# Delta-rule heads: values from keys times state, filling work in eighths, and two reordered GpSimd steps

## The reference, cut to what matters

```python
t_inv = triangular_solve(eye + lower, eye)            # inverse of a unit triangular matrix
u = t_inv @ v_beta
w = t_inv @ (k_beta * exp(g))
def step(state, xs):
    v_new = u_c - w_c @ state
    o = q_c @ state + qk_c @ v_new
    state = state * exp(g_last) + k_c.T @ v_new
```

## Time and profile before

| What | Value |
|---|---|
| median of 3 runs | 2177.07 us |
| the profiled execution, its own time | 2178.32 us |
| its span | 2176.5 us |
| mean granted TensorE clock | 0.989 |
| PE busy over the span | 97% |
| DVE, ACT, POOL busy | 60%, 39%, 19% |
| the heads' loop and the last head | about 75 to 627 us of the span |

### The profile page before, as it was taken

One profiled execution on the slowest core, in us unless ns is written; L12 is line 12 of the kernel. 1 busy time (PEld: TensorE's weight loads), 2 busy tenths in 40 slices (PEclk: granted clock), 3 DMA queues, 4 the chain that ended last, 5 costly groups with the idle time before them and its releaser, 6 DMA issues.

```text
span 2176.5 us, 29829 instructions
## 1 busy us (share of the span) xinstructions
PE 2120.2 (97%) x10312; PEld 1735.3 (80%) x10312; DVE 1315.0 (60%) x1907; ACT 858.1 (39%) x1352; POOL 421.0 (19%) x326
## 2 busy tenths in 40 slices
PE   6999999999999999999999999999999999999998
PEld 4788888888888878888888888888777777888886
DVE  6777887777644453333557655643788867555431
ACT  3333333333332232222335454422666735545321
POOL 0456765556700300000110000011000000000021
PEclk8999999999999999999999999999999999999999
DMA  7344433344333323333332333233221122333332
GB/s 286 97 117 125 116 101 111 106 116 125 106 88 116 116 78 96 96 96 93 96 114 69 96 96 96 86 102 101 59 59 49 54 84 85 96 96 96 94 96 73
DMA packets 394815, 216.81 MB, mean 100 GB/s; under 512 B 7880, under 2 KB 391298, under 8 KB 393219
## 3 DMA queue, kind: packets, MB, share of 16 engines
q1 hardware_dynamic: 393939, 213.51, 33.3%
q0 software_dynamic: 288, 2.10, 0.3%
q10 hardware_dynamic: 528, 0.40, 0.1%
HBM read 211.79 MB, written 4.19 MB: 99 GB/s over the span
## 4 chain that ended last, share of the span: by engine, by line
PE 74%; DVE 7%; issue 7%; POOL 5%; ACT 2%; POOLq 0%; DMA 0%; ACTq 0%; DVEq 0%
PE ps L2206 23%; PE ps L2208 22%; PE ps L2207 22%; POOL ada_w L725 3%; PE ps L2382 1%; DVE small L2088 1%; DVE a_sb L2121 1%; DVE w_lo L1309 1%; POOL gd_dia L748 1%; PE ps L2233 1%; DVE a_t_lo L2097 1%; ACT at_swap L1200 1%; DVE prob L2116 1%; POOL ada_s L725 1%; ACT prob L1223 0%
## 5 line engine op out<-in xcount | busy, mean ns | idle before, releaser
L2206 PE MATMUL ps<-h_hi,w_hi 128*128 128x512 f32 x1896 | 770.4, 406 | 7.1 <-DVE h_lo L1373 5.5
L2208 PE MATMUL ps<-h_hi,w_lo 128*128 128x512 f32 x1896 | 743.6, 392 | 0.0
L2207 PE MATMUL ps<-h_lo,w_hi 128*128 128x512 f32 x1896 | 741.9, 391 | 0.0
L1309 DVE TENSOR_TENSOR w_lo<-raw,w_hi 128x1024 fp32r<-128x1024 f32 x333 | 430.0, 1292 | 355.9 <-ACT w_hi L808 355.5
L808 ACT ACTIVATE w_hi<-raw 128x1024 fp32r<-128x1024 f32 x336 | 355.6, 1059 | 636.6 <-PE ps L2208 578.3
L2206 PEld LDWEIGHTS ps<-h_hi,w_hi 128*128 128x128 f32 x1896 | 358.6, 189 | 80.2 <-issue 13.8
L2208 PEld LDWEIGHTS ps<-h_hi,w_lo 128*128 128x128 f32 x1896 | 357.5, 189 | 78.2
L2207 PEld LDWEIGHTS ps<-h_lo,w_hi 128*128 128x128 f32 x1896 | 359.0, 189 | 65.0
L2206 PE MATMUL ps<-act_hi,w_hi 128*128 128x512 f32 x528 | 206.0, 390 | 0.0
L2208 PE MATMUL ps<-act_hi,w_lo 128*128 128x512 f32 x528 | 205.5, 389 | 0.0
L2207 PE MATMUL ps<-act_lo,w_hi 128*128 128x512 f32 x528 | 205.4, 389 | 0.0
(11 more groups left out here) (383 smaller groups left out, 2599.0 us busy)
## 6 DMA issues: line engine op xcount, KB each, us to landing
raw<-ffn_w_up SPq DMA_DIRECT2D x88, 512.0 KB, 3.7
raw<-w_in SPq DMA_DIRECT2D x72, 512.0 KB, 3.7
raw<-w_ffn_in SPq DMA_DIRECT2D x44, 512.0 KB, 3.7
ada_w<-w_ada SPq DMA_DIRECT2D x32, 512.0 KB, 3.8
raw<-ffn_w_down SPq DMA_DIRECT2D x32, 512.0 KB, 3.8
raw<-diff_w_qkv SPq DMA_DIRECT2D x24, 512.0 KB, 3.7
ada<-w_ada SPq DMA_DIRECT2D x8, 1024.0 KB, 12.6
ada_w<-w_ada_f SPq DMA_DIRECT2D x16, 512.0 KB, 3.7
```

The source lines that it names most:

```text
L1309: nc.vector.tensor_tensor(w_lo[:, tile.slot], raw[:, tile.raw], w_hi[:, tile.slot].bitcast(F32), SUB)\
L2206: nc.tensor.matmul(dst, w_hi[:, tile.slot, k], hi, start=first, stop=False)
L2207: nc.tensor.matmul(dst, w_hi[:, tile.slot, k], lo, start=False, stop=False)
L2208: return nc.tensor.matmul(dst, w_lo[:, tile.slot, k], hi, start=False, stop=last)
```

## The change

- **Values.** `w`, its four matmuls, ACT's copy of it and `k_beg` go. For chunks 1 to 3, PE multiplies the keys with the state (`k_state{n}`, one f32 matmul of its own), DVE adds the result times the (negative) factor to `v_b` (`rest{n}`), and `v_new{n}` is one matmul of the inverse with that. ACT copies the keys to `k_f` after `q_squares`.
- **Filling.** It goes by eighths (3 large matmuls). The steps keep what they had, two eighths, but for `v_new0` (it had two quarters, now two eighths), `o2` and `o3` (one eighth each, had a quarter), and the new `k_state{n}` (two eighths each).
- **DVE's queue.** The short convolution's taps move to places behind the states; `ahead(4)` moves from behind the third copy to behind the fourth and `short_gate`; `ahead(5)` moves from behind the fourth copy to behind `g_col`, ahead of `ahead(6)`.
- **POOL.** The fourth mask stands ahead of the second modulation tile.
- **The start.** DVE computes `w_lo` of head 0's tile 1. POOL does `k_norm` of head 0 first, then `w_lo` of tiles 2 and 3, and DVE waits for them only ahead of `ahead(0)`. Head 0 stands outside POOL's loop.

```diff
-    DVE_STEPS += ["k_dec"] if _n == 0 else ["u_pairs3", "k_beg"] if _n == 3 else []
-PE_STEPS += [f"u{LEVELS - 1}", "w"]
-ACT_STEPS += ["w"] + [f"o_squares{_n}" for _n in range(NC)] + ["o_hi"]
+    DVE_STEPS += ["k_dec"] if _n == 0 else ["u_pairs3"] if _n == 3 else []
+PE_STEPS += [f"u{LEVELS - 1}"]
+ACT_STEPS += [f"o_squares{_n}" for _n in range(NC)] + ["o_hi"]
 for _n in range(NC):
-    PE_STEPS += [f"v_new{_n}", f"o{_n}"]
-    DVE_STEPS += [f"v_new{_n}"] + ([f"state{_n}"] if _n < NC - 1 else [])
+    PE_STEPS += ([f"k_state{_n}"] if _n else []) + [f"v_new{_n}", f"o{_n}"]
+    DVE_STEPS += ([f"rest{_n}"] if _n else []) + [f"v_new{_n}"] + ([f"state{_n}"] if _n < NC - 1 else [])
...
-HEAD_FILL = {name: 1 for name in PE_STEPS}
-HEAD_FILL.update(y0=2, v_new0=2, o_turn=3)
-LAST_FILL = dict(HEAD_FILL, y1=2, y2=2, y3=2, y4=2, y5=2, v_new0=2, v_new1=2, v_new2=2, ada_turns=2)
+HEAD_FILL = {name: 2 for name in PE_STEPS}
+HEAD_FILL.update(y0=4, o2=1, o3=1, o_turn=6)
+LAST_FILL = dict(HEAD_FILL, y1=4, y2=4, y3=4, y4=4, y5=4, v_new0=4, v_new1=4, v_new2=4, ada_turns=4, o_turn=4, tail=16)
...
-            for tile in [QKVZ.tile(t, 0).ahead() for t in range(1, 4)]:
+            def first_splits():
+
+                for t in (2, 3):
...
                 nc.gpsimd.tensor_tensor(col4(S_KN), col4(S_KSS), minus_half, ALU.pow).then_inc(g_pool, 1)
+                if splits is not None:
+                    splits()
...
-                    if n in (1, 2):
-                        modulation(n - 1)
+                    if n in (1, 3):
+                        modulation(n // 2)
...
+                nc.scalar.activation(gd["k_f"][:], gd["k_s"][:], ACT.Copy).then_inc(g_act, 1)
...
-                after_pe("w")
-                nc.scalar.activation(gd["x_t"][:], bank(7), ACT.Copy).then_inc(g_act, 1)
...
+            split(QKVZ.tile(1, 0).ahead())
             z_silu(QKVZ, 3, 0, 0)
-            dve.wait_ge(lo_ready, QKVZ.tile(3, 0).ahead().before + 1)
...
                 for n in range(NC):
+                    if n:
+                        after_pe(f"k_state{n}")
+                        own("v_beta")
+                        nc.vector.scalar_tensor_tensor(part(gd["v_b"], n), part(bank(7), n), small[:, S_KBEG + n:S_KBEG + n + 1],
+                                                       part(gd["v_b"], n), MULT, ADD).then_inc(g_dve, 1)
                     after_pe(f"v_new{n}")
                     nc.vector.tensor_copy(part(gd["y_t"], n), part(bank(2), n)).then_inc(g_dve, 1)
                     if more and n == 0:
                         short_in()
-                        short_tap(0)
-                    if more and n == 1:
-                        short_tap(2)
-                    if more and n == 2:
-                        ahead(4)
-                    if more and n == 3:
-                        ahead(5)
...
-                    if more and n == 0:
-                        short_tap(1)
-                    if more and n == 1:
+                    if more and n < 3:
+                        short_tap(n)
+                    if more and n == 3:
                         short_gate()
+                        ahead(4)
...
                 if more:
+                    ahead(5)
                     ahead(6)
...
-                fill("w")
-                after_act(f"u{LEVELS - 1}")
...
-                by_chunk(7, gd["k_beg"], u_t).then_inc(g_pe, 1)
-
                 for n in range(NC):
+                    if n:
+                        fill(f"k_state{n}")
+                        after_dve(f"state{n - 1}")
...
+                        nc.tensor.matmul(part(bank(7), n), part(gd["k_f"], n), state[:], start=True, stop=True).then_inc(g_pe, 1)
                     fill(f"v_new{n}")
-                    v_new = nc.tensor.matmul(part(bank(2), n), part(u_t, n), part(gd["v_b"], n), start=True, stop=n == 0)
                     if n:
-                        after_act("w")
-                        after_dve(f"state{n - 1}")
-                        v_new = nc.tensor.matmul(part(bank(2), n), part(x_t, n), state[:], start=False, stop=True)
+                        after_dve(f"rest{n}")
+                    else:
+                        after_act(f"u{LEVELS - 1}")
+                    v_new = nc.tensor.matmul(part(bank(2), n), part(u_t, n), part(gd["v_b"], n), start=True, stop=True)
```

More of the change, by code:

```diff
@@ L172 @@
              "u_diag", "x_pairs", "qk"]
-ACT_STEPS = ["k_squares", "exp_decay", "exp_g", "exp_g_rows", "exp_last", "exp_left", "q_squares"]
+ACT_STEPS = ["k_squares", "exp_decay", "exp_g", "exp_g_rows", "exp_last", "exp_left", "q_squares", "k_copy"]
 POOL_STEPS = ["k_norm"] + [f"mask{_n}" for _n in range(WHOLE_LEVELS)] + ["low_pairs", "ada", "o_norm"]
@@ L348, in block_kernel @@
         names = ["q_s", "k_s", "v_s", "z_g", "th", "cc", "dec", "low_d", "low", "q_g", "u_t", "x_t",
-                 "y_t", "k_beg", "k_dec", "v_b", "dia"]
+                 "y_t", "k_f", "k_dec", "v_b", "dia"]
         gd = {n: sb("gd_" + n, [P, T], at=work + 2048 * j) for j, n in enumerate(names)}
@@ L711, in _, with head @@
             factor(N_MIX)
-            pool.wait_ge(g_dve, 1)
-            for tile in [QKVZ.tile(t, 0).ahead() for t in range(1, 4)]:
[L715 to L720, removed]
+            def first_splits():
+                for t in (2, 3):
+                    tile = QKVZ.tile(t, 0).ahead()
+                    pool.wait_ge(hi_ready, tile.before + 1)
+                    pool.wait_ge(lo_ready, tile.before)
+                    nc.gpsimd.tensor_tensor(w_lo[:, tile.slot], raw[:, tile.raw], w_hi[:, tile.slot].bitcast(F32), SUB)\
+                      .then_inc(lo_ready, 1)
+            def head(h, splits=None):
                 own = [24 * h + 1]
@@ L767, in _ @@
             pool.sem_inc(ada_own, 1)
-            with pool.Fori(0, H) as h:
+            head(0, first_splits)
+            with pool.Fori(1, H) as h:
                 head(h)
@@ L1060, in head @@
                                          accum_out=small[:, S_OSQ + n:S_OSQ + n + 1]).then_inc(g_act, 1)
-                    if more and n == 0:
-                        ahead(5)
+                    if n == 0:
+                        if more:
+                            ahead(5)
+                        else:
+                            second_gate(3)
                 if more:
@@ L1622, in head @@
                 qk.then_inc(g_dve, 1)
+                dve.wait_ge(lo_ready, stage.tile(0, i).ahead().before)
                 ahead(0)
@@ L1685, in head @@
                         k_dec.then_inc(g_dve, 1)
[L1686 to L1689, removed]
                     if more and n == 1:
@@ L2208, in term, with eighth @@
                 return nc.tensor.matmul(dst, w_lo[:, tile.slot, k], hi, start=False, stop=last)
+            def eighth(stage, t, i, k):
+                tile = stage.tile(t, i)
+                if k == 0:
+                    pe.wait_ge(lo_ready, tile.before + 1)
+                    open_out(stage.out(t, i))
+                last = term(bank(stage.banks[t]), tile, k, h_hi[:, k], h_lo[:, k], k == 0, k == KD - 1)
+                if k == KD - 1:
+                    last.then_inc(tile_done, 1)
             def quarter(stage, t, j, i, q):
@@ L2366, in fill @@
                     for _ in range(fills.get(name, 0)):
-                        t, q = divmod(filled[0], 4)
-                        quarter(stage, t, t, i, q)
+                        t, k = divmod(filled[0], KD)
+                        eighth(stage, t, i, k)
                         filled[0] += 1
```

16 lines of the change are left out of this document (7 added, 9 removed).

## The result

The changed kernel takes 2185.99 us (median of 6 runs, 2183.4 to 2187.3), the kernel before 2177.59 (6 runs, 2175.9 to 2179.3) in the same comparison. The ratio is 1.0039, with a 95% interval of 1.0027 to 1.0050: slower by 8.4 us, 0.39%. The forecast was 2187.7 and slower, with a range of 2167 to 2192. The profiled execution took 2186.86 us, with a span of 2185.1.

A forecast was written before the change was run, and what follows sets the result against it. PE, busy 97%, was taken to bound the kernel. Seven heads at +1.7 us (+11.9), head 0 -0.3 and last head -1.05 gave +10.6: 2188.9 us for the profiled execution, 2187.7 for the median, range 2167 to 2192.

The forecast's parts named there:

- What PE saves: PE's matmuls in each head: fewer to issue with the same tile work, 1.05 us less a head, 8.4 in eight.
- The last head: Final head, with no next convolution to make DVE late: it keeps the savings, 1.05 us.
- The wait at o0: PE ahead of o0: waits 1.4 us for DVE's copy behind conv_silu, making v_new3 1.5 us later a head.
- Level 4: DVE's w_lo behind POOL's multiplication: ends where it did, so earlier mask and missing k_beg gain nothing; winning gives 0.7 us.
- The loads: DMA chain from v_new3 on: o_turn waits about 0.45 us, next x0 comes 0.2 us later a head.
- Head 0: Start of the first head: earlier norm, but POOL's splits delay the pair decay; gains 0.3 us, 2.4 without blocking.
- The sum: Whole kernel: seven heads +11.9 us, head 0 -0.3, last head -1.05, in all +10.6.
- The two new waits: At o0 and in the load chain behind v_new3: +1.5 and +0.2 us a head; chance of this forecast 0.55.
- the clock case: Rival: the wait at o0 also lowers PE's clock, 2 us more in each of seven heads, 2202 us; chance 0.08.
- the middle: Rival: DVE in time for o0 and the DMA chain holds, within 0.2%, about 2178 us; chance 0.17.
- the faster case: Rival: neither wait appears, DVE in time and loads with 0.5 us to spare, 2164 us; chance 0.17.

The follow-up runs named there:

- the fastest version: Changed kernel with four eighths of filling at v_new0, ahead(4), ahead(5) behind third, fourth copies, conv_silu(2) behind v_new0's copy, values' first tap behind u5's copy: 2163.57 us.
- the silu behind the copy: Changed kernel with DVE's conv_silu(2) moved from in front of v_new0's copy to right behind it: 2178.47 us, ratio 0.9998.
- the mask alone: Kernel before the change with only POOL's fourth mask put ahead of its second modulation tile: 2177.14 us, ratio 0.9993.
- the splits back: Changed kernel with DVE's ahead(4) and ahead(5) back behind the third and fourth value copies, filling unchanged: 2178.71 us, ratio 1.0000.
- the cover: Changed kernel with two eighths of filling moved from ahead of o_turn to ahead of v_new0: 2184.65 us, ratio 1.0029.
- the old start: Changed kernel with POOL again computing remainders of head 0's tiles 1 to 3 ahead of its heads, DVE waiting, norm behind: 2186.83 us, ratio 1.0037.
- the short modulation: Changed kernel with POOL's modulation multiplication and first two additions cut to 2 of 128 columns, leaving most of the sum out: 2168.79 us, ratio 0.9959.
- the version with both: Changed kernel with ahead(4), ahead(5) back behind the third and fourth copies and two eighths of filling moved from o_turn to v_new0: 2167.68 us, ratio 0.9949.
- the version with the splits back and the silu behind: Changed kernel with ahead(4), ahead(5) back behind the third and fourth copies and conv_silu(2) right behind v_new0's copy: 2170.45 us, ratio 0.9963.

## Why the prediction was right, point by point

**What PE saves.** Predicted 1.05 us a head, "with the same tile work". This term was too large: in the fastest version, where PE never waits, it is 0.77 (u5 to the next x0, above). The tile work is the same but cut into more fillings. A quarter with a step of its own costs 1.48 us; the quarter that the cover adds to the filling ahead of v_new0 costs 1.36 (from u5 to v_new0 3.46 us with it, 2.10 in the changed kernel). The change has two fillings more, three for `k_state{n}` less the one of w, and at 0.12 each that is 0.24 of the missing 0.28, an estimate. The last head, where DVE has no next convolution, is 1.03 shorter (from x0 to the output's first product 70.39 us, 71.42 before), but that isn't a clean measure of the matmuls: up to u5 it takes 0.28 longer (29.89, 29.61 before), and a wait of 0.22 ahead of o2 that the kernel before has in it is gone. That it came out at the 1.05 predicted is luck.

**The wait at o0.** Predicted 1.4, and the view of waits has 1.17, put down to the copy as said; o0 comes 2.94 us behind v_new0, which is 1.33 more than the 1.61 that it takes where it doesn't wait (the silu behind the copy). From u5 to o0 the distance fell by 2.30 (7.34 before, 5.04 now) where the prediction's numbers give 2.2, and from o0 to v_new3 it is 13.45 us where it said 13.3. The cause was tested from both sides: it goes with more cover, with the silu behind the copy, and with POOL's work taken away.

**Level 4.** Here a term was mis-sized. "I count the mask and the missing `k_beg` at nothing", because w_lo "behind a POOL instruction that starts at about 115.8" ends where it ended. The mechanism held: w_lo ends 1.09 behind POOL's multiplication, and the gain at y3 turned into the wait at u5 (0.53), which I had not named as a wait. But the multiplication itself moves. In head 2 of the changed kernel, whose x0 stands at 229.76, POOL and PE have

```profile
247.43 1.90 POOL L724 TENSOR_TENSOR ada_w<-ada_w,cact 128x1024 f32<-128x1024 f32 x1
253.25 0.68 PE L2418 MATMUL ps<-gd_u_t,gd_y_t 128*64 128x64 f32 x8 [0.53 <-DVE gd_y_t L1645]
```

So POOL starts it 17.67 us behind x0, and u5 comes at 23.49. With the mask alone it is 17.67 and 23.49 too, and before it was 17.88 and 23.72. The shift of u5, 0.23, is that of POOL's start, 0.21, and all of it comes with the mask's place. (Head 1 of the changed kernel has 17.49 and 23.32 and isn't typical.) From u5 to v_new3 the distance grew by 1.53 us (16.96 before, 18.49 in head 1), as the predicted 1.5; u5's earlier start brings the growth of x0 to v_new3 down to 1.31 (40.69 to 42.00, heads 2 to 6). The early mask could have been worth more than was taken for it: where u5 doesn't wait, in the fastest version, u5 comes 0.87 us earlier than before.

**The loads.** Predicted +0.2 on v_new3 to x0, measured +0.31, with ACT's splits waiting for the DMA, o_turn for the gate copy (0.3 to 0.5 us, 1.28 in head 0, where 0.45 was predicted) and x0 for DVE's copy. That what PE saves there "is waited away" was shown by the splits back (23.91) and by the cover, which took 1.5 us of filling away and moved x0 by nothing.

**Head 0.** Predicted 0.3 us earlier, measured 54.43 - 54.04 = 0.39, with one step of it wrong, so the agreement is in part luck. "PE's wait of 4.25 us for the norm's product shrinks to about 1.9" came out as 3.52. `kss` came early, as said, but the small product behind it, which PE needs, met POOL's first split. Timeline of DVE and POOL at the start of head 0, the changed kernel:

```profile
82.13 0.17 DVE L1588 TENSOR_SCALAR small<-small 128x4 f32<-128x4 f32 x1 [5.46 <-ACT gd_y_t L994]
...
83.53 2.18 DVE L1598 SCALAR_TENSOR_TENSOR small<-small,b_tok 128x4 f32<-128x4 f32 x1
...
87.39 1.71 DVE L1611 TENSOR_TENSOR gd_u_t<-gd_low_d,cst 128x512 f32<-128x512 f32 x1
...
83.36 5.19 POOL L716 TENSOR_TENSOR w_lo<-raw,w_hi 128x1024 fp32r<-128x1024 f32 x2
```

L1598 works on 4 elements of a partition and takes 2.18 us; with the old start it takes 0.17. The step that failed is in the order on POOL, not in the time of its splits: counted from the first matmul of h_hi, which stands at 43.47 in the kernel before and 41.53 here, they were placed at 42.03 (85.5) and began at 41.83 (83.36). They follow the norm at once, where POOL did nothing behind it before, and the prediction had them run over q_g and the pair decay but left out the small product L1598, which DVE reaches 0.17 us behind their start. The pair decay (L1611) was blocked too, 1.71 for 0.69, and ended 47.57 us behind the first matmul of h_hi, where it was 48.28 before and 47.85 with the old start: some tenths are left of 2.4 us, as worked out, but by two blocked instructions and not by one. The Trainium skill ("SBUF — State Buffer", section "SBUF: two separate sides") says that the one of the two engines that comes second is blocked for the whole of the other's instruction; the 2.18 us and the short modulation's return to 0.68 and 1.22 agree with it.

**The sum.** Seven heads +11.02 (predicted +11.9), head 0 -0.39 (-0.3), the last head -1.03 (-1.05): +9.6 against +10.6. The two new waits and their sizes hold; what PE saves and the place of u5 were sized wrong, by 0.28 and 0.2 us a head. What PE saves hardly touches the sum of the seven heads, where DVE and the loads set the pace. The spans of the two profiled executions differ by 8.6, since the first matmul of h_hi stands 1.94 us earlier in that of the changed kernel and the rest behind the last head is 0.94 longer; I don't put the first to the change, as the other kernels with the same start have that matmul between 40.9 and 44.2, nor the second, since nothing is edited there; this is argued, not tested.

**The rivals.** The clock stayed at 1.00 in the loop, so the clock case is out. DVE was not in time for o0, and the chain of loads didn't hold, so the middle and the faster case are out for the change as it stands. The faster one's time (2164) is what the version reaches that makes its conditions true (2163.57), though by other terms: it added 1.05 for the matmuls and 0.5 for the mask in each head, and they measure 0.77 and, up to u5, 0.87.

## What to carry to other kernels

When matmuls leave a chain, the cover that they gave leaves with them: look at what stands in the other engine's queue ahead of the result that is now needed earlier, and put that result first. Two waits in one period hide each other, so an edit that gains hardly anything alone can be worth 10 us beside another: after each fix read again which chain ends last. An instruction that is late because one of the other engine is running moves with that one's start, so predict that start too. Count the pieces into which filling work is cut as well, not its amount alone.

## What the runs showed of the hardware

- DVE instructions of very different sizes were caught by a POOL instruction: 128x4 took 2.18 us instead of 0.17, 128x512 took 1.77 instead of 0.68, 128x1024 2.65 instead of 1.22. The first tap of the short convolution (L1561, a TENSOR_SCALAR, which has one tensor and a factor for each partition as inputs) was caught too: 2.15 us in head 1 of the changed kernel, 0.04 behind the start of a multiplication on POOL (192.12), and 0.49 with the short modulation. Where POOL's start is known too, `w_lo` ended 1.08 and 1.09 us behind the end of POOL's instruction, so the price is the wait plus nearly its whole own time.
- A wait on PE delays its step by more than the wait shown: from y0 to x0 it is 2.27 us without a wait (160.55 to 162.82) and 2.67 with one of 0.22 (227.09 to 229.76). That x0 is then 0.10 longer as well (1.15 instead of 1.05), but it can be that without any wait shown (97.90 in the earlier trace rows).
- In head 0 the clock falls in some executions and not in others at nearly the same wait. Windows of 84 to 90 us in steps of 2, the changed kernel (a wait of 3.52 us) and the version with the splits back (3.26): length, PE's busy us, clock, DMA share, GB/s.

```profile
84.00:86.00 2.00, 0.23 (x1) 0.55 0.00 0
86.00:88.00 2.00, 2.00 (x8) 0.50 0.51 127
88.00:90.00 2.00, 2.00 (x9) 0.50 0.65 156
```

```profile
84.00:86.00 2.00, 0.00 (x0) 1.00 0.02 7
86.00:88.00 2.00, 0.74 (x6) 1.00 0.00 0
88.00:90.00 2.00, 2.00 (x12) 1.00 0.85 226
```

  The first falls to 0.50, the level of 1.2 GHz, the second stays at 1.00, that of 2.4 GHz. From the norm's product to x0 of head 0 it is then 9.80 us in the first and 9.45 in the second, and 10.07 in the version with both, which has the same code there, a wait of 3.28, and fell: a fall cost 0.35 and 0.62 us there. In the fastest version (a wait of 3.41) the clock fell too, from 86.5 us on, and it has 9.45 as well: where the clock stays up, PE waits for POOL's first mask there (1.39 us at 92.41 in the version with the splits back and the silu behind), and the slower matmuls fit into that wait. The Trainium skill ("TensorE: Matmul & The Clock Gate", Part 1) says that the number of slow matmuls varies between runs of one kernel, at its start; these traces, in mid-kernel, are of the same kind, though each is of another version. From the first matmul of h_hi to x0 of head 0 the nine versions with the new start and the full modulation take 52.59 to 54.33 us, and much of that spread arises ahead of the norm's product. Differences of this size at the start of head 0, the 0.39 above too, are therefore not safe from one execution each.
